# Two pairs of lanes, the second two steps behind the first, in the neighbourhood attention of a long fused kernel

## The reference, cut to what matters

```python
s_win = s_win.reshape(b, h, GRID_W, kr * NA_KC) * scale + bias[None]   # 8 grid rows in reach, 16 of 64 columns
s_ctx = jnp.einsum('bhwd,blhd->bhwl', qr, kc) * scale                  # 256 context keys
p = jax.nn.softmax(jnp.concatenate([s_win, s_ctx], axis=-1), axis=-1)
return einsum('bhwrc,brwchd->bwhd', p_win, v_win) + einsum('bhwl,blhd->bwhd', p_ctx, vc)
```

## Time and profile before

| | |
|---|---|
| median of 3 executions | 3404.7 us (3401.68 to 3418.88) |
| profiled execution | 3405.37 us, of which its span 3403.2 us |
| PE busy in the span | 3128.7 us (92%) |
| DVE, ACT busy | 1703.8 us (50%), 1154.4 us (34%) |
| granted PE clock, mean | 0.948 of full |

### The profile page before, as it was taken

How to read it: one execution, slowest core, us unless ns; L and a number is a source line. 1 busy time by engine, 2 the same in 40 slices (tenths; PEclk the granted TensorE clock), 3 DMA queues, 4 the chain that set the end, 5 groups by cost and what they waited for, 6 DMA issues and landing times.

```text
span 3403.2 us, 38707 instructions
## 1 busy us (share of the span) xinstructions
PE 3128.7 (92%) x15522; PEld 2475.0 (73%) x15522; DVE 1703.8 (50%) x2760; ACT 1154.4 (34%) x1858; POOL 141.5 (4%) x145
## 2 busy tenths in 40 slices
PE   7999889899998889999999999669999879987997
PEld 6888567666667778888788887348888757877886
DVE  5434543456655654344744346874535455335235
ACT  3223133344444333223332224453323233333332
POOL 0000000211211100000000000000000000000000
PEclk9999899799999999999999999669999989998999
DMA  3333132000000033232223332003232210201231
GB/s 127 99 93 95 58 111 77 27 28 28 27 28 14 1 120 102 94 99 93 81 93 100 99 99 78 1 1 117 93 95 91 69 37 1 79 19 47 81 97 59
DMA packets 173895, 234.76 MB, mean 69 GB/s; under 512 B 14201, under 2 KB 111062, under 8 KB 173462
## 3 DMA queue, kind: packets, MB, share of 16 engines
q1 hardware_dynamic: 173718, 232.29, 21.5%
HBM read 228.05 MB, written 4.19 MB: 68 GB/s over the span
## 4 chain that ended last, share of the span: by engine, by line
PE 82%; DVE 10%; ACT 4%; issue 2%; POOL 1%; DMA 0%; SPq 0%; DVEq 0%; ACTq 0%
PE banks L810 62%; PE banks L1240 3%; PE banks L930 2%; PE banks L921 1%; PE banks L1228 1%; PE banks L1234 1%; PE banks L965 1%; PE banks L992 1%; PE banks L898 1%; PE banks L988 1%; PE banks L939 1%; DVE diff_scores L2220 1%; DVE diff_small L2226 1%; PE banks L876 1%; DVE kv_tmp L1869 1%
## 5 line engine op out<-in xcount | busy, mean ns | idle before, releaser
L1780 DVE TENSOR_TENSOR weights_lo<-weights_raw,weights_hi 128x1024 fp32r<-128x1024 f32 (+2 forms) x393 | 472.9, 1207 | 1035.0 <-ACT weights_hi L1308 1033.5
L810 PE MATMUL banks<-operand_hi,weights_hi 128*128 128x512 f32 x2208 | 872.7, 395 | 34.2 <-DVE weights_lo L1780 14.6
L810 PE MATMUL banks<-operand_lo,weights_hi 128*128 128x512 f32 x2208 | 865.6, 392 | 0.0
L810 PE MATMUL banks<-operand_hi,weights_lo 128*128 128x512 f32 x2208 | 865.4, 392 | 0.0
L1308 ACT ACTIVATE weights_hi<-weights_raw 128x1024 fp32r<-128x1024 f32 (+2 forms) x393 | 407.9, 1041 | 1089.4 <-PE banks L810 1049.5
L810 PEld LDWEIGHTS banks<-operand_hi,weights_hi 128*128 128x128 f32 x2208 | 418.3, 189 | 130.3 <-issue 32.4
L810 PEld LDWEIGHTS banks<-operand_lo,weights_hi 128*128 128x128 f32 x2208 | 418.7, 190 | 88.2 <-issue 2.2
L810 PEld LDWEIGHTS banks<-operand_hi,weights_lo 128*128 128x128 f32 x2208 | 418.1, 189 | 88.4
L930 PE MATMUL banks<-operand_lo 128*128 128x512 f32 x370 | 173.2, 492 | 1.3 <-ACT v L1423 1.3
L810 PE MATMUL banks<-hidden_ffn_hi,weights_hi 128*128 128x512 f32 x352 | 137.1, 390 | 0.0
L810 PE MATMUL banks<-hidden_ffn_lo,weights_hi 128*128 128x512 f32 x352 | 136.9, 389 | 0.0
(11 more groups left out here) (497 smaller groups left out, 4412.5 us busy)
## 6 DMA issues: line engine op xcount, KB each, us to landing
weights_raw<-in_ffn_w_in_dram SPq DMA_DIRECT2D x352, 256.0 KB, 2.9
weights_raw<-in_ffn_w_out_dram SPq DMA_DIRECT2D x88, 512.0 KB, 3.6
weights_raw<-in_w_in_dram SPq DMA_DIRECT2D x36, 512.0 KB, 3.6
weights_raw<-in_rwkv_w_rkv_dram SPq DMA_DIRECT2D x24, 512.0 KB, 3.6
weights_raw<-in_w_mod_dram SPq DMA_DIRECT2D x24, 512.0 KB, 4.9
weights_raw<-in_w_kv_dram SPq DMA_DIRECT2D x16, 512.0 KB, 3.5
weights_raw<-in_rwkv_w_o_dram SPq DMA_DIRECT2D x8, 512.0 KB, 5.2
weights_raw<-in_diff_w_q_dram SPq DMA_DIRECT2D x8, 512.0 KB, 4.6
```

The costliest lines, as they stand in the source:

```text
L810: mm = nc.tensor.matmul(o, l, r, start=first and t == 0 and job["opens"], stop=last and t == 2, **skip)
L1780: nc.vector.tensor_tensor(ring_lo[0:p, u["slot"], 0:n, 0:w], ring_raw[0:p, u["ring"], 0:n, 0:w], f32(ring_hi[0:p, u["slot"], 0:n, 0:w]), A ...
```

## The change

A list of its own orders the "na" attention. Lanes 0 and 1 are the first pair, lanes 2 and 3 the second, and in every turn the first pair makes its step and the second pair the step that the first made two turns ago. Every engine takes its order from this list. In "na" the row maximum moves from step 1 to step 0, right behind the bias of the same lane. In both attentions the reciprocal moves from step 2 to step 4, in front of DVE's wait for the product with the values. The MLA attention keeps its order of lanes.

```diff
+PAIR_LAG = 2
+def in_pairs(tasks, steps):
+    order = []
+    for turn in range(tasks // 4 * steps + PAIR_LAG):
+        for pair in range(2):
+            group, step = divmod(turn - pair * PAIR_LAG, steps)
+            if 0 <= group < tasks // 4:
+                order += [(4 * group + 2 * pair + e, 2 * pair + e, step) for e in range(2)]
+    return order
...
-        ATTN_ORDER = woven(MLA_HEADS, 5 * TB, LANES, False)
+        ATTN_ORDER = {"mla": woven(MLA_HEADS, 5 * TB, LANES, False), "na": in_pairs(NA_HEADS, 5 * TB)}
...
-                for hd, lane, s in ATTN_ORDER:
+                for hd, lane, s in ATTN_ORDER[name]:
...
+            def row_maximum(name, hd, lane, tb, scale):
+                sm, flat = attn_small[:, lane], ps[:, 2 * lane:2 * lane + 2].rearrange("p a b -> p (a b)")
+                nc.vector.tensor_reduce(sm[:, 0:1], flat[:, 0:KEYS], AX_X, ALU.max).then_inc(*dve_own.by())
+                dve.wait_ge(*dve_own.now())
+                nc.vector.tensor_scalar(sm[:, 1:2], sm[:, 0:1], -scale, None,
+                                        ALU.mult).then_inc(*lane_dve[lane].by((name, "max", hd, tb)))
...
                                                 ALU.add).then_inc(*own.by((name, "bias", hd, tb)))
-                    elif s == 1:
-                        if name == "na":
-                            dve.wait_ge(*own.at((name, "bias", hd, tb)))
-                        else:
-                            dve.wait_ge(*lane_pe[lane].at((name, "s", hd, tb)))
-                        nc.vector.tensor_reduce(sm[:, 0:1], flat[:, 0:KEYS], AX_X, ALU.max).then_inc(*dve_own.by())
-                        dve.wait_ge(*dve_own.now())
-                        nc.vector.tensor_scalar(sm[:, 1:2], sm[:, 0:1], -scale, None,
-                                                ALU.mult).then_inc(*own.by((name, "max", hd, tb)))
-                    elif s == 2:
-                        dve.wait_ge(*lane_act[lane].at((name, "exp", hd, tb)))
-                        nc.vector.reciprocal(sm[:, 3:4], sm[:, 2:3]).then_inc(*own.by((name, "rs", hd, tb)))
+                        dve.wait_ge(*own.at((name, "bias", hd, tb)))
+                        row_maximum(name, hd, lane, tb, scale)
+                    elif s == 1 and name != "na":
+                        dve.wait_ge(*lane_pe[lane].at((name, "s", hd, tb)))
+                        row_maximum(name, hd, lane, tb, scale)
                     elif s == 3 and tb % 2 == 0:
...
                     elif s == 4:
+                        dve.wait_ge(*lane_act[lane].at((name, "exp", hd, tb)))
+                        nc.vector.reciprocal(sm[:, 3:4], sm[:, 2:3]).then_inc(*own.by((name, "rs", hd, tb)))
                         dve.wait_ge(*lane_pe[lane].at((name, "o", hd, tb)))
```

More of the change, by code:

```diff
@@ L535, in attention_plan @@
                 elif s == 2:
-                    lane_dve[lane].expect((name, "rs", hd, tb))
                     lane_pe[lane].expect((name, "turn", hd, tb))
@@ L541, in attention_plan @@
                     lane_pe[lane].expect((name, "o", hd, tb))
+                    lane_dve[lane].expect((name, "rs", hd, tb))
                     lane_dve[lane].expect((name, "o", hd, tb))
-        attn_lane = {hd: lane for hd, lane, s in ATTN_ORDER}
         attention_plan("mla")
```

## The result

The changed kernel takes 3458.7 us in the median of its executions (3440.2 to 3475.5), the kernel before 3403.2 beside it; the ratio is 1.0124, with a 95% interval of 1.0074 to 1.0175. So the change costs 1.0 to 1.2%. I had forecast slower by 0.6% and 3436 as the top of the range; the direction was right, the size was not: even the two shorter of the four executions, 3440.2 and 3446.8, lie above that range.

A forecast was written before the change was run, and what follows sets the result against it. In neighbourhood attention, a 3.35 us PE gap in a round and matmuls at 1.2 GHz lose the time. 145.2 + 10.4 - 133.6 less 0.7 gave +21.3 us on 3405.4, stated as 3426, range 3412 to 3436.

The forecast's parts named there:

- part 1: Neighbourhood attention, order of pairs: rounds of 17.8 us with a 4.6 us PE gap, stage 145.2 us at full clock, 19.6 more.
- the pieces: Full-clock times read from the second round: bias and maximum 3.54 a pair, transposes 1.77, products with the values 2.7 us.
- the sum: Whole kernel: 145.2 + 10.4 - 133.6 = +22.0 us, less 0.7 for MLA, +21.3.
- part 2: PE clock in neighbourhood attention: a 1.2 GHz stretch in all eight rounds, costing 10.4 us in all.
- 1.3 x 8: Neighbourhood attention: 1.3 us lost in each of eight low-clock stretches, about 4 us of PE time each, 10.4 us.
- Both 1.5 times as long: At 1.2 GHz a transpose takes 0.224 us against 0.147, a pass of the values product 0.167 against 0.112.
- 18 as a bound: Upper bound on the clock loss, all products and transposes after each gap slow: 8 x (1.33 + 0.92) = 18 us.
- part 3: MLA attention, late reciprocal: copies start earlier, 0.18 us off each of four rounds, 0.7 us in all.
- What costs nothing: Neighbourhood attention: SP's bias loads for heads 6 and 7, ready by 22 us and needed at 26.6, cost nothing.
- the pairs cover each other: Rival: PE has other work during each bias and maximum; stage about 100 us, kernel 3372; chance 0.10 together with a no-change case.
- cut-up idle time would spare the clock: Rival: the order costs as forecast, but the clock loses no more than now or less; kernel 3416 to 3424; chance 0.20.
- the clock wouldn't come back between gaps: Rival: all scores, transposes and products slow, 7.5 us more a round; stage 205 us, kernel 3476; chance 0.04.

## Why the prediction was wrong in size

**The order, part 1: right.** Both kinds of round, the engine, the lanes and the line behind which PE stands are as written, 4.6 us of gap against 4.63 measured, released eight times by the copy L2393. That the copy's place is the cause is shown twice, by a later bias and by a copy on ACT, both 120.4 us. Their rounds also bear out the pieces (7.14 against 7.06). The pieces put the order's share of the loss at 19.6 us (19.8 with the 8 x 15.67 = 125.4 in place of the sum's 125.6); it is not measured apart from the clock, as no kernel here has a gap of 4.6 us without slow stretches.

**The clock, part 2: the term that failed.** The forecast put 10.4 us on it, "1.3 x 8", from two numbers, and both were too small. The stage took 175.7 - 145.2 = 30.5 us more than the pieces at full clock.

First the price. "Both 1.5 times as long" is wrong: at 1.2 GHz passes of the products and of the transposes take about twice as long. For the product, "0.33 / 2 = 0.167" was mis-sized: 24 passes after a gap took 5.38, that is 0.224 each, against 0.112. I had read the price from the first two steps of a product in the last 0.4 us of a low stretch. The passes there start at 3097.59, 3097.70 and 3097.92: the first step is 0.11, but the second was 0.21 already. Three more low stretches of that trace end in the first passes of a product (from 3114.63, 3131.68 and 3148.74), and all three show 0.11 and then 0.21. For the transposes I compared 24 back to back (5.38 / 24) with a lane's six, 0.88 / 6 = 0.147, which hold a start and an end of their own. Inside the six, passes start 0.11 apart, and in the low stretch 0.21. In a row of twelve behind a product, a pair's transposes take 1.47 us at full clock (the kernel with wide products) and 2.77 at 1.2 GHz (row at 3079.33 of the changed kernel's trace).

Then the amount. I had put about 4 us of PE work into each of eight stretches, 32 us, which is what the trace of before has; the changed kernel's nine have 69.

The ledger from the chain: the eight products behind a gap took 5.38, 5.38, 5.22, 5.16, 5.38, 5.38, 5.08 and 5.02, 42.0 us against 21.6, so 20.4 more; the transposes behind them 19.7 against the 14.2 of the pieces, 5.5 more; the remaining 4.6 of 30.5 us are put down to slow scores and the slow transposes of the first round. Since a pair's transposes in a row take 1.47 and not the pieces' 1.77, up to 8 x 0.3 = 2.4 us of the 145.2 may belong to the clock as well; that is an estimate. I had 18 as a bound; with 0.224 for a pass of the product the same bound is 8 x (2.7 + 0.92) = 29, close to what came.

The Trainium skill ("TensorE: Matmul & The Clock Gate", section Terms) charges half of the throttled time, which I had weighed and set aside. The rows bear it out: 0.224 for 0.112 in the products, 0.21 for 0.11 in the transposes, and half of the 69 us of work at 1.2 GHz is 35, an estimate that lies near the 30.5 of the ledger.

**MLA, part 3: right in kind, too small.** 1.8 us came off, not 0.7. I took away only the wait that the wait row shows. In the chain an even round also ran through the reciprocal and the copy, and its products began 0.18 after the last lane's transposes (2854.96 against 2853.91 + 0.87). Now they begin 0.10 before the end of these. With the ends, the chain has 5.57 us for the products where it now has 5.31: 0.26 and 0.17 more, 0.43 a round, four times. The sum had only the 0.18.

**What costs nothing: right.** SP's and POOL's loads of the bias never held a lane.

**The rivals.** That the pairs cover each other is false for this change and true one edit away from it, though the stage of about 100 us that the rival named came only with the scores between the transposes (100.5). That cut-up idle time would spare the clock is refuted: the low time doubled, and in the lockstep kernel with the early maximum gaps of 2.23 us and less came with more low time (56 us) than gaps of 3.35 (38). That the clock wouldn't come back between gaps was given 0.04; it came back each time, but late.

**Still open:** how long or how often PE must idle for its clock to fall. Gaps of 2.2 us did it in some rounds and not in others, and with the same gaps the kernel before had 38 us of low time in one execution and 44 in another. Open too is why some rounds stayed at 1.2 GHz through a whole product and others did not, and whether the wider products helped by their columns or by the moment at which a stretch began.

## What to carry to other kernels

When an interleaving is laid down by one list for all engines, write out each engine's queue and look for the instruction that another engine waits for standing behind one that waits for that other engine; here the cure was to let one engine run the same list one step later. After a gap, ask which matmuls come first: their price at the low clock must be read from a stretch of many passes, and a price from two records at the edge of a stretch is none. Compare passes in a row with passes in a row: a short group carries its own start and end. Cut the traces at the same points before believing a total: 27 of 65 us were not the change's.

## What I had not expected of the hardware

Back-to-back products of 64 columns on 128x128 weights ran for 10.1 us at 1.2 GHz without getting the clock back, in three rounds of the lockstep kernel with the early maximum. The Trainium skill ("TensorE: Matmul & The Clock Gate", Part 1) says that activity releases the throttle; in these rounds 10.1 us of it did not, and the clock came back only in the work behind. With 128 columns no stretch passed 6.8 us in two kernels, one execution each.

A pair's product takes nearly the same time with 128 columns as with 64, at either clock (2.94 and 2.89 at 2.4 GHz, 5.49 and 5.38 at 1.2).

In the changed kernel's chain one bias is put down to POOL's masking (3130.31 + 2.09 = 3132.40). It is a coincidence of ends: the masking that ended there is another head's. The bias of the head in question had been masked 13 us earlier, and the scores that it needed ended at 3132.4 as well. So nothing is to be gained there.
